# Up-projections of the last feed-forward part as seven block products on halves of 256 columns

## The chip, the cores and the metric

The program runs on one core of a Trainium2 chip. A core has TensorE (PE, matrix products; its weight loads are shown apart as PEld), VectorE (DVE), ScalarE (ACT), GpSimd (POOL) and SyncE (SP, which here only issues DMA transfers). The engines run side by side, each strictly in the order of its own instruction list, and wait for each other through semaphores. The metric is the device time of one execution in microseconds, median of three runs. One execution was also profiled; all rows come from that one.

## The reference

Two layers of a diffusion backbone over 512 latent tokens and 256 context tokens, width 1024, in float32. Each layer is a half feed-forward part, a token mixer, and a second half feed-forward part. The last part of the last layer runs on the 512 latent tokens alone:

```python
def half_ffn(x, shift, scale, gate, w_in, w_out, g, b):
    h = modulate(x, shift, scale)
    a, u = jnp.split(h @ w_in, 2, axis=-1)
    y = (jax.nn.silu(a) * u) @ w_out
    return layernorm(ALPHA * x + 0.5 * gate * y, g, b)
...
        x_lat = half_ffn(x_lat, m_lat[6], m_lat[7], m_lat[8], ffn_w_in[l, 1], ffn_w_out[l, 1], ln_g[l, 2], ln_b[l, 2])
```

`w_in` is 1024 x 5632 and `w_out` 2816 x 1024. 2816 is 22 chunks of 128.

## The kernel before

**Tiling.** Activations are kept transposed: 128 features on the partitions, 8 chunks of features (`KC`), tokens along the free dimension. Every operand of a product is split into a high and a low part (`HHI`, `HLO` for the activations, `WHI*`, `WLO*` or `WSH`, `WSL` for weights), and a product of one 128 x 128 weight block is three matmuls: high x high, high x low, low x high (`product`, L3103 to 3111). ACT makes the high parts by a copy that rounds, DVE the low parts by a subtraction.

**Feed-forward parts.** There are four, `ffn0` to `ffn3`. Each has eleven iterations (`FI`), and each iteration has a unit A and a unit B (one chunk of 128 hidden features each, gate and up). A unit is: the up-projection on PE, silu on ACT, the multiplication by the up half on DVE, and the split into `GHI`, `GLO`. The down-projection of iteration i-1 runs in iteration i; DVE adds each of its results into `X` (`accumulate`).

**The last part, `ffn3`, before.** It uses the plain form (`ffn`, with S = 1). Per iteration PE runs up A (48 matmuls of 512 columns), the whole down-projection (8 groups of 6 matmuls, 512 columns) and up B (48). Weights come in six transfers of 512 KB per iteration through two raw buffers (`RAW[0]`, `RAW[1]`, printed as RAW): transfer q may be issued when transfer q-2 has been split (`lo_done`).

**The other three parts** use the block form (`wide`). In iterations 2 to 10 the up-projection of a unit, an [8 chunks of features] x [768 tokens] product with two outputs (gate, up), is cut into halves in all three directions and computed by seven block products instead of eight (`seventh`: 4 k-steps x 3 matmuls on 384 columns each), with sums of activation blocks (`TH_`, `TL_`, made once per part in iterations 0 to 2) and with mixes of weight blocks, made per unit. Each unit's results are put together on DVE (`second_sum`, `gate_first`, `third_sum`, `fourth_sum`, `up_second`, `up_first`, `gate_second`). The weights for the next unit are made while this one runs, in one buffer `WSH`/`WSL` of seven places:

- DVE mixes in place in the raw buffers: `difference`, `total`, `mix_second`, `last_mix` (L2220 to 2248), 512 columns each.
- ACT makes the high parts: `raw_hi` (1024 columns, L1246), four `mix_hi` (L1253) and `second_hi` (L1259), 512 columns each.
- DVE makes the low parts: `low_first` (1024 columns, L2217) and five of 512 columns, the last being `low_last` (L2256), which frees both raw buffers at once (`lo_done` + 2).

The raw buffers are used in turn by a half of `w_out` rows (`rows_load`, L736), then the first and the second half of the next unit's up weights (`unit_load`, L714). The rows and the first half may be issued when `low_last` of the unit before is done; the second half uses the buffer of the rows, so it is issued when DVE has split the rows (L1802, called `rows()` in `unit`). Down-projections are spread: half of the groups after unit A, half after unit B. The order on each engine is written out by hand in `unit` and `body` of each engine's block.

Of the kernel before, what the change touches and what calls it, by code (L numbers as in the profile page):

```python
# [167 lines left out]
def build(nc, A, out):  # L168
# [197 lines left out]
    RST = sb("RST", [P, LAT // P], at=r2 + 8192)  # L366
    OUT = sb("OUT", [P, LAT // P, D], F32, at=w_at)
# [93 lines left out]
    ffn_plan("ffn3", 1)  # L461
# [91 lines left out]
    BLOCKS = {"ffn0": 0, "ffn1": 1, "ffn2": 2}  # L553
# [18 lines left out]
    def fourth_sums(name, k):  # L572

        return T4S[k][:, :, :] if name == "ffn2" else HL32[:, 2 * k:2 * k + 2, HALF:TOK]

    def blocks_of(part):

        H = (HHI, HLO)[part]
        T = (TH_, TL_)[part]
        return {"11": lambda k: H[:, k, 0:HALF], "21": lambda k: H[:, 4 + k, 0:HALF], "22": lambda k: H[:, 4 + k, HALF:TOK],  # L580
                "T4": lambda k: H[:, k, HALF:TOK], "T1": lambda k: T[1][k // 2][:, k % 2, :],
                "T2": lambda k: T[2][k // 2][:, k % 2, :], "T3": lambda k: T[3][k // 2][:, k % 2, :]}
# [13 lines left out]
    def half_bank(a, m):  # L596

        return PS[(1, 0)[m - 4] if a == 0 and m in (4, 5) else (6, 7, 2, 5)[m % 4]][:, 0:CTX]
# [87 lines left out]
    def _(sp):  # L686
# [28 lines left out]

        def ffn(name, w_in, w_out):
            q0 = plan[name].q
            for half in range(2):
                ffn_load(w_in, w_out, "A", 0, half, q0 + half)

            def body(i, last=False):
                for slot, d, half, j in ffn_halves(last):
                    ffn_load(w_in, w_out, slot, i + d, half, q0 + j, i)
            with sp.Fori(0, FI - 1) as i:
                body(i)
            body(FI - 1, last=True)
# [145 lines left out]
        ffn("ffn3", A["ffn_w_in"][1, 1], A["ffn_w_out"][1, 1])  # L872
# [216 lines left out]
    def _(act):  # L1089
# [57 lines left out]
        def ffn(name, S, ada, nxt):  # L1147
            p = plan[name]

            used = {"A": (p.A, S), "B": (p.B, S), "W": (p.W, KC * S)}  # L1150

            def free_value(slot, u):
                base, per = used[slot]
                if isinstance(u, int) and base + per * u == 0:
                    return None
                return base + per * u

            def silus(slot, i):

                b = 0 if slot == "A" else 3  # L1160
# [33 lines left out]
            for e, s in enumerate(ORDER[2]):  # L1194
# [4 lines left out]
                if e == 0:  # L1199
                    next_unit(nxt, "A")  # L1200
# [2777 lines left out]
```

## Time and profile before

| | us |
|---|---|
| median of three runs | 2800.71 (2800.42 to 2800.82) |
| the profiled execution | 2798.63 |
| its span, first to last instruction | 2796.9 |
| PE busy | 2767.4 (99%) |
| DVE busy | 1988.9 (71%) |
| ACT busy | 1041.6 (37%) |

A row of a timeline gives start, duration, engine, line, operation and operands; in brackets the idle time of the engine just before, and what ended it. A matmul's duration is longer than the distance to the next one, since they are pipelined, so the cost of a matmul in a dense stretch is the distance between starts. The same holds, by less, for DVE and ACT. Iterations 1 to 10 of `ffn3` lie between about 2440 and 2766.5 us of the span, and the steady half-iterations of `ffn2`, the block form without other work in it, at about 1700 to 1950 us.

### The profile page before, as it was taken

To read this page: it belongs to the slowest core of one execution; us is meant where nothing else is said; L and a number is where in the kernel's file an instruction comes from. 1 tells how busy PE (TensorE), PEld (TensorE's weight loads), DVE (VectorE), ACT (ScalarE), POOL (GpSimd) and SP (SyncE) were. 2 spreads that over 40 slices of the span, in tenths; PEclk is the share of its full clock that TensorE was granted. 3 is DMA by queue.
4 is the path that set the end of the run, shared out by engine and by line. 5 is a ranking of instruction groups with operands and counts; after the bars stand their busy time and mean duration, and the time that the engine had idled before them with its cause. 6 is when DMAs were issued, how large, how long until landed. Compare 5 with 4: busy or idle time off the path is not lost.

```text
span 2796.9 us, 46107 instructions
## 1 busy us (share of the span) xinstructions
PE 2767.4 (99%) x17150; PEld 2423.9 (87%) x17150; DVE 1988.9 (71%) x3249; ACT 1041.6 (37%) x1646; POOL 296.2 (11%) x404
## 2 busy tenths in 40 slices
PE   8999999999999999999999999999999999999999
PEld 4899989988868889999898999999978998988888
DVE  5786777776785777667677877777767886655555
ACT  4232323346632523323234333333356665522221
POOL 2000000011101000000001000000105554000000
PEclk9999999999999999999999999999999999999999
DMA  9344342222222243443421112222311101232221
GB/s 340 106 158 158 120 142 68 68 68 76 69 102 84 77 156 129 157 152 125 142 83 43 56 69 70 72 71 71 86 43 26 27 21 46 85 119 95 100 90 61
DMA packets 112292, 268.00 MB, mean 96 GB/s; under 512 B 30760, under 2 KB 40876, under 8 KB 112045
## 3 DMA queue, kind: packets, MB, share of 16 engines
q1 hardware_dynamic: 89164, 185.62, 20.5%
q0 software_dynamic: 22144, 77.61, 7.8%
q10 hardware_dynamic: 864, 3.15, 0.3%
q8 instruction: 79, 1.29, 0.2%
q14 instruction: 41, 0.33, 0.0%
HBM read 259.52 MB, written 5.24 MB: 95 GB/s over the span
## 4 chain that ended last, share of the span: by engine, by line
PE 93%; DVE 3%; ACT 2%; DMA 1%; issue 1%; POOL 0%; ACTq 0%; DVEq 0%; POOLq 0%; SPq 0%
PE PSALL L3109 15%; PE PSALL L3110 15%; PE PSALL L3111 15%; PE PSALL L3399 9%; PE PSALL L3400 9%; PE PSALL L3401 9%; PE PSALL L3185 2%; PE PSALL L3024 2%; PE PSALL L3186 2%; PE PSALL L3187 2%; PE PSALL L3862 2%; PE PSALL L3847 1%; PE PSALL L3138 1%; PE PSALL L3808 1%; PE PSALL L3810 1%
## 5 line engine op out<-in xcount | busy, mean ns | idle before, releaser
L2146 DVE SCALAR_TENSOR_TENSOR X<-PSALL,GATE,X 128x512 f32<-128x512 f32 x480 | 280.1, 612 | 94.5 <-PE PSALL L3111 94.5
L3399 PE MATMUL PSALL<-HHI,WSH 128*128 128x384 f32 x864 | 291.2, 337 | 0.0
L3400 PE MATMUL PSALL<-HLO,WSH 128*128 128x384 f32 x864 | 290.2, 336 | 0.0
L3401 PE MATMUL PSALL<-HHI,WSL 128*128 128x384 f32 x864 | 289.8, 335 | 0.0
L1253 ACT ACTIVATE WSH<-RAW 128x512 fp32r<-128x512 f32 x216 | 136.6, 632 | 228.7 <-DVE RAW L2223 152.6
L3399 PE MATMUL PSALL<-TH,WSH 128*128 128x384 f32 x648 | 220.3, 340 | 0.0
L3401 PE MATMUL PSALL<-TH,WSL 128*128 128x384 f32 x648 | 218.9, 338 | 0.0
L3400 PE MATMUL PSALL<-TL,WSH 128*128 128x384 f32 x648 | 218.9, 338 | 0.0
L3109 PE MATMUL PSALL<-GHIA,WHIW 128*128 128x512 f32 (+1 forms) x570 | 198.5, 348 | 0.6 <-DVE X L2146 0.6
L3110 PE MATMUL PSALL<-GLOA,WHIW 128*128 128x512 f32 (+1 forms) x570 | 196.6, 345 | 0.0
L3111 PE MATMUL PSALL<-GHIA,WLOW 128*128 128x512 f32 (+1 forms) x570 | 196.0, 344 | 0.0
L3111 PE MATMUL PSALL<-GHIB,WLOW 128*128 128x512 f32 (+1 forms) x570 | 195.8, 343 | 0.0
L3109 PE MATMUL PSALL<-GHIB,WHIW 128*128 128x512 f32 (+1 forms) x570 | 195.7, 343 | 0.0
L3110 PE MATMUL PSALL<-GLOB,WHIW 128*128 128x512 f32 (+1 forms) x570 | 195.6, 343 | 0.0
L3109 PE MATMUL PSALL<-HHI,WHIA 128*128 128x512 f32 (+1 forms) x464 | 167.2, 360 | 0.0
L3110 PE MATMUL PSALL<-HLO,WHIA 128*128 128x512 f32 (+1 forms) x464 | 165.3, 356 | 0.0
L3111 PE MATMUL PSALL<-HHI,WLOA 128*128 128x512 f32 (+1 forms) x464 | 165.3, 356 | 0.0
L3399 PEld LDWEIGHTS PSALL<-HHI,WSH 128*128 128x128 f32 x864 | 162.3, 188 | 0.4 <-issue 0.4
L3400 PEld LDWEIGHTS PSALL<-HLO,WSH 128*128 128x128 f32 x864 | 162.5, 188 | 0.0
L3401 PEld LDWEIGHTS PSALL<-HHI,WSL 128*128 128x128 f32 x864 | 162.2, 188 | 0.0
L3109 PE MATMUL PSALL<-HHI,WHIB 128*128 128x512 f32 (+1 forms) x432 | 155.9, 361 | 0.0
L3111 PE MATMUL PSALL<-HHI,WLOB 128*128 128x512 f32 (+1 forms) x432 | 154.6, 358 | 0.0
(443 smaller groups left out, 6829.6 us busy)
## 6 DMA issues: line engine op xcount, KB each, us to landing
RAW<-in_ffn_w_in_dram SPq DMA_DIRECT2D x174, 512.0 KB, 3.8
ADA<-in_ada_w_dram POOLq DMA_DIRECT2D x128, 512.0 KB, 5.6
RAW<-in_ffn_w_out_dram SPq DMA_DIRECT2D x88, 512.0 KB, 3.6
RAW<-in_ev_w_in_dram SPq DMA_DIRECT2D x20, 512.0 KB, 3.7
ADAF<-in_ada_w_dram POOLq DMA_DIRECT2D x16, 512.0 KB, 12.0
WRAW<-in_mla_w_q_up_dram SPq DMA_DIRECT2D x16, 288.0 KB, 3.1
RAW<-in_ev_w_out_dram SPq DMA_DIRECT2D x8, 512.0 KB, 4.5
RAW<-in_mla_w_in_dram SPq DMA_DIRECT2D x8, 512.0 KB, 4.0
```

Of the source, the lines that this page charges most:

```text
L1253: return act.activation(WSH[:, place, :], raw[:, 512 * cols:512 * cols + 512], ACT.Copy)
L2146: dve.scalar_tensor_tensor(X[:, m, lo:lo + n], down_bank(m, s, 2), GATE[:, j, m, s:s + 1], X[:, m, lo:lo + n], ALU.mult, ALU.add).then_inc ...
L3024: x = te.matmul(PS[bank][32 * j:32 * j + 32, 0:D // 4], SC[:, k, :], rows[:, j * D // 4:(j + 1) * D // 4], start=(k == 0), stop=(k == KC - 1))
L3109: te.matmul(out, w_hi, x_hi(k), start=(k == 0), stop=False)
L3110: te.matmul(out, w_hi, x_lo(k), start=False, stop=False)
L3111: x = te.matmul(out, w_lo, x_hi(k), start=False, stop=(k == ks - 1))
L3185: te.matmul(out, hi, HHI[:, k, lo:lo + n], start=(k == 0), stop=False)
L3186: te.matmul(out, hi, HLO[:, k, lo:lo + n], start=False, stop=False)
L3187: return te.matmul(out, low, HHI[:, k, lo:lo + n], start=False, stop=(k == KC - 1))
L3399: te.matmul(out, w_hi, hi[block](k), start=(k == 0), stop=False)
L3400: te.matmul(out, w_hi, low[block](k), start=False, stop=False)
L3401: x = te.matmul(out, w_lo, hi[block](k), start=False, stop=(k == 3))
```

## The change

`ffn3` takes the block form in iterations 2 to 10, on halves of 256 columns instead of 384. Iterations 0 and 1 stay plain (`up_classic`). The plain `ffn` functions are replaced on every engine by `narrow`, which follows `wide` line by line, without the context tokens; SP uses `wide` as it is. Down-projections keep 512 columns and are spread, four groups after each unit. The high part of the gated result moves from DVE to ACT. In the last iteration the down rows get a third buffer of their own (`WL3H`, `WL3L`).

```diff
-    ffn_plan("ffn3", 1)
+    stage("ffn3", q=6 * FI, A=2 * FI, B=2 * FI, W=KC * FI, evac=KC * FI, g=FI, gB=FI, gs=2 * FI)
...
-        ffn("ffn3", A["ffn_w_in"][1, 1], A["ffn_w_out"][1, 1])
+        wide("ffn3", A["ffn_w_in"][1, 1], A["ffn_w_out"][1, 1])
...
+            def unit(slot, i, rows, q):
...
+                first_copy(slot, i)
+                rows()
+                silu_first(slot, i)
+                raw_hi(n, q, i, (g_pe, 5 * v + 3))
+                mix_hi(n, 1, 2, first, 0, (g_pe, 5 * v + 4)).then_inc(g_hi, 1)
+                mix_hi(n, 2, 3, second, 0, (g_pe, 5 * v + 5)).then_inc(g_hi, 1)
+                second_hi(n, q, i, (pe[slot], used + 1))
+                silu_second(slot, i)
+                mix_hi(n, 3, 4, second, 1, (g_pe, 5 * v + 2)).then_inc(g_hi, 1)
+                mix_hi(n, 4, 5, first, 1, (pe[slot], used + 2)).then_inc(hi_done, 2)
...
+                def low_first():
+                    dve.wait_ge(g_hi, 5 * n + 1)
...
+                def difference():
+                    dve.wait_ge(raw_in[raw_slot(q + 1)], raw_value(q + 1, i))
+                    dve.wait_ge(g_lo, 5 * n + 1)
+                    dve.tensor_tensor(first[:, left], first[:, left], second[:, left], ALU.subtract).then_inc(g_mix, 1)
...
+            def up(slot, i, q):
...
+                te.wait_ge(mul[slot], p.gs + 2 * i)
+                te.wait_ge(g_lo, 5 * v + 1)
+                seventh(0, "11", b).then_inc(g_pe, 1)
+                te.wait_ge(g_lo, 5 * v + 5)
+                te.wait_ge(t_lo, 8 * blk + 6)
+                seventh(4, "T2", b + 1).then_inc(g_pe, 1)
+                seventh(1, "21", b + 2).then_inc(g_pe, 1)
+                te.wait_ge(g_p1, v + 1)
+                seventh(2, "T3", b).then_inc(g_pe, 1)
+                te.wait_ge(g_add, 7 * v + 1)
+                seventh(3, "T1", b + 1).then_inc(g_pe, 1)
+                te.wait_ge(g_add, 7 * v + 2)
+                te.wait_ge(t_lo, 8 * blk + 7)
+                seventh(6, "T4", b + 2, lambda: te.wait_ge(t_lo, 8 * blk + 8)).then_inc(pe[slot], 1)
+                te.wait_ge(g_add, 7 * v + 3)
+                te.wait_ge(lo_done, q + 2 + 6 * i)
+                seventh(5, "22", b).then_inc(pe[slot], 1)
...
+                for m in groups:
+                    if m >= 2:
+                        te.wait_ge(evac, p.evac + KC * i + m - 1)
...
+            def body(i):
+                up("A", i, wide_q(name, "A", 1) - 6)
+                down(i - 1, range(0, 4), wide_q(name, "W0", 1) + 6 * i - 6 + 1)
+                up("B", i, wide_q(name, "B", 1))
+                down(i - 1, range(4, 8), wide_q(name, "W1", 1) + 6 * i + 1)
```

The order on VectorE, iteration 1 of `ffn3` before, from the multiplication of unit B on (GM, GHI, GLO are the gated result and its parts, WLOB, WLOA low parts of weights, RAW_54 and RAW_53 the two raw buffers, X the residual stream):

```order
L1990 TENSOR_TENSOR GMB<-GMB,PSALL 128x512 [waits silu_B,ln_x]
L2000 CAST GHIB<-GMB 128x512 [waits mul_B]
L2002 TENSOR_TENSOR GLOB<-GMB,GHIB 128x512 [waits ghi_B]
L1802 TENSOR_TENSOR WLOB<-RAW_54,WHIB 128x1024 [waits hi_done]
L2015 SCALAR_TENSOR_TENSOR X<-PSALL,GATE,X 128x512 [waits pe_W]
L1802 TENSOR_TENSOR WLOB<-RAW_53,WHIB 128x1024 [waits hi_done]
L1990 TENSOR_TENSOR GMA<-GMA,PSALL 128x512 [waits silu_A]
L2015 SCALAR_TENSOR_TENSOR X<-PSALL,GATE,X 128x512 [waits pe_W] x3
L1802 TENSOR_TENSOR WLOA<-RAW_54,WHIA 128x1024 [waits hi_done]
```

And in the changed kernel, the same engine in unit A of the last iteration, which has the order of the steady ones, from the split of the rows to the end of the weights for the next unit (seven_hi, seven_mix the counts of high parts and mixes, raw_in1 the landing of a transfer):

```order
L1873 TENSOR_TENSOR WLOW<-RAW_54,WHIW 128x1024 [waits hi_done]
L2101 TENSOR_TENSOR GMA<-PSALL,P_95 128x256 [waits seven_pe]
L2156 TENSOR_TENSOR WSL<-RAW_53,WSH 128x1024 [waits seven_hi]
L2110 TENSOR_TENSOR U_96<-PSALL,GMA 128x256 [waits seven_add,seven_pe,mul_B]
L2162 TENSOR_TENSOR RAW_53<-RAW_53,RAW_54 128x512 [waits seven_lo,raw_in1]
...
L2141 TENSOR_TENSOR GMA<-PSALL,GMA 128x256 [waits pe_A]
L2183 TENSOR_TENSOR RAW_54<-RAW_54,RAW_53 128x512 [waits seven_mix,seven_lo]
L2187 TENSOR_TENSOR RAW_53<-RAW_53,RAW_54 128x512 [waits seven_mix]
L2146 TENSOR_TENSOR GMA<-GMA,P_95 128x256 [waits silu_A]
L2077 SCALAR_TENSOR_TENSOR X<-PSALL,GATE,X 128x512 [waits evac,pe_W] x2
L2191 TENSOR_TENSOR WSL<-RAW_54,WSH 128x512 [waits seven_hi]
L2077 SCALAR_TENSOR_TENSOR X<-PSALL,GATE,X 128x512 [waits evac,pe_W]
L2195 TENSOR_TENSOR WSL<-RAW_53,WSH 128x512 [waits hi_done]
```

Where each weight tile was split by itself, there is now one chain of mixes and splits, and accumulations of the down-projection stand between its last members. On SyncE the loop of `ffn3` issued, for each iteration, two transfers for unit B, two for unit A and two of rows:

```order
L714 ISA [waits lo_done]
L714 DMA RAW_54<-in_ffn_w_in_dram 128x1024
...
L714 DMA RAW_53<-in_ffn_w_in_dram 128x1024
...
L714 DMA RAW_54<-in_ffn_w_in_dram 128x1024
...
L714 DMA RAW_53<-in_ffn_w_in_dram 128x1024
...
L714 DMA RAW_54<-in_ffn_w_out_dram 128x1024
```

In the loop of the changed kernel each unit's pair is followed by one transfer of rows:

```order
L717 ISA [waits lo_done]
L717 DMA RAW_53<-in_ffn_w_in_dram 128x1024
...
L717 DMA RAW_54<-in_ffn_w_in_dram 128x1024
...
L727 DMA RAW_53<-in_ffn_w_out_dram 128x2x512
...
L717 DMA RAW_54<-in_ffn_w_in_dram 128x1024
...
L717 DMA RAW_53<-in_ffn_w_in_dram 128x1024
```

So the second transfer of each pair takes the buffer that the rows before it held.

## Rows read from the trace of the kernel before

**Rows 1.** The page: span, busy times, granted clock by slice, the chain's engines.

```profile
span 2796.9 us, 46107 instructions
PE 2767.4 (99%) x17150; PEld 2423.9 (87%) x17150; DVE 1988.9 (71%) x3249; ACT 1041.6 (37%) x1646; POOL 296.2 (11%) x404
...
PEclk9999999999999999999999999999999999999999
...
PE 93%; DVE 3%; ACT 2%; DMA 1%; issue 1%; POOL 0%; ACTq 0%; DVEq 0%; POOLq 0%; SPq 0%
```

**Rows 2.** Busy times of 100 us inside `ffn3` (stretch, length, busy, granted clock, DMA).

```profile
2500.00:2600.00 100.00, 100.00 (x443) 82.84 (x442) 48.19 (x60) 20.99 (x24) 0.00 (x0) 1.00 0.31 101
```

**Rows 3.** PE timeline: 512-column matmuls in `ffn3`, the first and the 56th.

```profile
2559.81 0.39 PE L3109 MATMUL PSALL<-HHI,WHIB 128*128 128x512 f32 x1
...
2572.28 0.39 PE L3110 MATMUL PSALL<-HLO,WHIA 128*128 128x512 f32 x1
```

**Rows 4.** PE timeline: last down-projection; 256-column matmuls, the first and the 24th.

```profile
2766.53 0.28 PE L3299 MATMUL PSALL<-GHIA,WHIW 128*128 128x256 f32 x1
...
2771.55 0.28 PE L3109 MATMUL PSALL<-GHIA,WHIW 128*128 128x256 f32 x1
...
2774.31 0.28 PE L3111 MATMUL PSALL<-GHIB,WLOW 128*128 128x256 f32 x1
```

**Rows 5.** DVE timeline of `ffn2`, one half-iteration of the block form.

```profile
1860.20 0.68 DVE L2256 TENSOR_TENSOR WSL<-RAW,WSH 128x512 fp32r<-128x512 f32 x1
...
1868.11 1.22 DVE L1802 TENSOR_TENSOR WLOW<-RAW,WHIW 128x1024 fp32r<-128x1024 f32 x1
...
1873.45 0.68 DVE L2223 TENSOR_TENSOR RAW<-RAW,RAW 128x512 f32<-128x512 f32 x1
1874.05 0.56 DVE L2179 TENSOR_TENSOR GMA<-PSALL,GMA 128x384 f32<-128x384 f32 x1
...
1880.59 1.40 DVE L2146 SCALAR_TENSOR_TENSOR X<-PSALL,GATE,X 128x512 f32<-128x512 f32 x2
1881.91 0.68 DVE L2252 TENSOR_TENSOR WSL<-RAW,WSH 128x512 fp32r<-128x512 f32 x1
1882.51 0.87 DVE L2146 SCALAR_TENSOR_TENSOR X<-PSALL,GATE,X 128x256 f32<-128x256 f32 x2
1883.30 0.68 DVE L2256 TENSOR_TENSOR WSL<-RAW,WSH 128x512 fp32r<-128x512 f32 x1
```

**Rows 6.** ACT and SP timelines of the same half-iteration.

```profile
1865.90 1.05 ACT L1144 ACTIVATE WHIW<-RAW 128x1024 fp32r<-128x1024 f32 x1
...
1861.06 0.38 SPq L736 DMA_DIRECT2D RAW<-in_ffn_w_out_dram  x1
...
1869.50 0.33 SPq L714 DMA_DIRECT2D RAW<-in_ffn_w_in_dram  x1
```

**Rows 7.** Time from issue to landing, 1650 to 2000 us: rows, then up weights.

```profile
DMA to landing us min/median/max: 3.5/3.7/4.7
...
DMA to landing us min/median/max: 3.4/3.8/4.5
```

**Rows 8.** DVE groups by shape, from 2420 us on.

```profile
L2015 DVE SCALAR_TENSOR_TENSOR X<-PSALL,GATE,X 128x512 f32<-128x512 f32 x80 | 58.4, 748 | 22.8 <-PE PSALL L3111 22.8
...
L1919 DVE TENSOR_TENSOR X<-X,PSALL 128x256 f32<-128x256 f32 x16 | 5.9, 414 | 1.0 <-PE PSALL L3128 0.7 <-PE PSALL L3146 0.4
```

**Rows 9.** PE timeline of the kernel's start, around an idle time of 3.4 us.

```profile
16.23 1.08 PE L3024 MATMUL PSALL<-ADAF,SC 128*32 128x256 f32 x8 [3.40 <-DMA ADAF<-in_ada_w_dram]
...
20.95 0.73 PE L3024 MATMUL PSALL<-ADAF,SC 128*32 128x256 f32 x8
...
26.15 0.64 PE L3024 MATMUL PSALL<-ADAF,SC 128*32 128x256 f32 x8
```

More of the change, by code:

```diff
@@ L552, in build @@
     UNITS = 2 * (FI - 2)
[L553 removed]
+    BLOCKS = {"ffn0": 0, "ffn1": 1, "ffn2": 2, "ffn3": 3}
     def wide_q(name, kind, i):
@@ new lines, in unit @@
+            def unit(slot, i, q, rows, groups):
+                low_first, difference, total, low_difference, low_total, low_second, mix_second, last_mix, low_third, low_last = weights(q, i, seven(name, slot, i) + 1)
+                second_sum(slot, i)
+                rows()
+                gate_first(slot, i)
+                low_first()
+                third_sum(slot, i)
+                difference()
+                fourth_sum(slot, i)
+                up_second(slot, i)
+                total()
+                low_difference()
+                up_first(slot, i)
+                low_total()
+                gated_first(slot, i)
+                low_second()
+                gate_second(slot, i)
+                mix_second()
+                last_mix()
+                gated_second(slot, i)
+                for e in groups[:2]:
+                    accumulate(i - 1, e)
+                low_third()
+                accumulate(i - 1, groups[2])
+                low_last()
+                accumulate(i - 1, groups[3])
@@ new lines, in narrow @@
+            low_first, difference, total, low_difference, low_total, low_second, mix_second, last_mix, low_third, low_last = weights(wide_q(name, "A", 1), 1, seven(name, "A", 2))
+            accumulate(0, 0)
+            accumulate(0, 1)
+            block_sum(1, 1)
+            accumulate(0, 2)
+            block_sum(1, 3)
+            accumulate(0, 3)
+            block_sum(1, 2)
+            for n in (1, 3, 2):
+                block_difference(1, n)
+            low_first()
+            difference()
@@ L2116, in wide @@
+            for m in range(KC):
+                center(then, 1, 1, m)
         def wide(name, j, ada, t0, then, nxt, tables=None):
@@ new lines, in up_classic, with seventh @@
+                x.then_inc(pe[slot], 2)
+            def seventh(place, block, bank, half_way=None):
+                out = PS[bank][:, 0:CTX]
+                for k in range(4):
+                    w_hi, w_lo = (t[:, place, P * k:P * k + P] for t in (WSH, WSL))
+                    if half_way and k == 2:
+                        half_way()
+                    te.matmul(out, w_hi, hi[block](k), start=(k == 0), stop=False)
+                    te.matmul(out, w_hi, low[block](k), start=False, stop=False)
+                    x = te.matmul(out, w_lo, hi[block](k), start=False, stop=(k == 3))
+                return x
@@ L3363, in wide @@
+            sums(then, 1, 1, lambda m: e0 + KC + m + 1)
         def wide(name, ada, ln, then):
```

627 lines of the change are left out of this document (355 added, 272 removed).

## The prediction

> **What bounds the kernel now.** I read the page first: PE is busy 99% of the span, the granted clock reads full in every slice, and the chain that ended last is 93% PE [rows 1]. Then the stretch that the change touches: for 100 us inside `ffn3` PE is busy all the time, DVE 48%, ACT 21%, the DMA engines 31% [rows 2]. So here the number of matmuls, times the distance between two of them, is the time. The next view is the PE timeline, read for distances: 512 columns cost (2572.28 - 2559.81) / 55 = 0.2267 us [rows 3], 256 columns (2774.31 - 2771.55) / 23 = 0.1200 us [rows 4]. One iteration is 3 x 48 matmuls of 512 columns, 32.64 us, or 16.32 us for a half-iteration (one unit and half of a down-projection). The nine iterations that the change rewrites take 18 x 16.32 = 293.8 us and end where the last down-projection starts, at 2766.53 [rows 4].
>
> The second place to read is the steady part of `ffn2`, since it is the form that `ffn3` takes over. One half-iteration there runs from 1860.20 to 1883.30, the two starts of `low_last`: 23.10 us [rows 5]. What matters is not that PE is full there too, but the loop that runs beside it, below.
>
> **What the change takes from PE.** A unit was 48 x 0.2267 = 10.88 us; it becomes 7 x 12 = 84 matmuls of 256 columns, 84 x 0.1200 = 10.08 us. The down-projection keeps 24 x 0.2267 = 5.44 us per half-iteration. PE's work per half-iteration falls from 16.32 to 15.52 us, by 0.80; over 18 it is 14.4 us. Halving the columns saves 12.5% of the columns, but each matmul costs 0.013 us beyond its columns (twice 0.1200 less 0.2267), and there are 84 instead of 48, which leaves 7%.
>
> The Trainium skill, "TensorE: Matmul & The Clock Gate", section "Back-to-back issue gap", gives N/2.4 + 2.5 ns as the isolated distance of one matmul of N columns, which would be 109 and 216 ns; an estimate from it is a saving of 1.2 us per half-iteration, 21.6 us in all. Rows 3 and 4 show 120 and 227 ns for these split products, and the measured distances decide.
>
> **What it adds beside PE.** DVE work per half-iteration, in distances between starts: 256 columns 0.335 (duration 0.414 [rows 8], less the 0.08 by which an operation overlaps the next: 1873.45 to 1874.05 is 0.60 for a duration of 0.68 [rows 5]), 512 columns 0.60, 1024 columns 1.14, an accumulation 0.66 (1.40 for two, less the same 0.08 [rows 5]). Nine block sums and multiplications 3.0, four mixes and five low parts 5.5, two low parts of 1024 columns 2.3, four accumulations 2.7, the low part of the gated result 0.6: 14.1 us. Below 15.5, so as work it fits; ACT fits easily (some 8 us). What does not fit is the order.
>
> **The loop.** The weights of the next unit pass through two raw buffers, and each step waits for the one before. Followed once around, from the end of `low_last`:
> 1. SP issues the rows: 1861.06 against 1860.20 + 0.68 = 1860.88, so 0.18 us [rows 5, 6]. Landing takes 3.5 at least, 3.7 in the median [rows 7]: I take 3.6.
> 2. ACT makes the high part of the rows, 1.05 [rows 6]; DVE the low part, 1.22 [rows 5]. With 0.05 before each, 2.37.
> 3. That frees the buffer for the second half of the next weights: issued at 1869.50 against 1868.11 + 1.22, 0.17 [rows 5, 6], landing 3.4 at least, 3.8 in the median, for one alone less than for one of two in flight [rows 7]: I take 3.55. With steps 1 and 2: 0.18 + 3.6 + 2.37 + 0.17 + 3.55 = 9.9 us in which DVE can't go on to `difference`.
> 4. From `difference` to the end of `low_last` DVE goes through its list: 1873.45 to 1883.98, 10.53 us [rows 5]. Six of these operations have 384 columns (0.555 for the `fourth_sum`, [rows 5]) and will have 256 (0.414 [rows 8]), 0.14 less each, 0.8 in all; two accumulations of 256 columns (0.79 apart, 1882.51 to 1883.30 [rows 5]) become one of 512 (0.66). That gives 9.6.
> 5. Before `low_last` stands the accumulation of the third down group. In the changed kernel this group may start only when the first is accumulated (`evac`, one bank pair): first accumulation 0.75 [rows 8], group 1.36, pipeline end 0.16, against 1.92 that DVE needs to get there. DVE waits about 0.4.
>
> The loop is 9.9 + 9.6 + 0.4 = 19.9 us. It does not depend on PE's speed. In `ffn2` the same count gives 9.9 + 10.5 = 20.4, and PE needs 23.1, so it is hidden; there ACT starts on the rows only at 1865.90 [rows 6], well after they landed, as it first waits for PE. In `ffn3` PE needs 15.5, and the loop becomes the pace: +3.6 us per half-iteration against 16.32, where 0.80 was to be won. PE will wait in two places: before the seventh block product, which needs `third_sum`, queued on DVE behind `low_first`, which needs the rows split and the gate sum (about 1.2 us), and before the third down group, whose bank waits for an accumulation that is queued behind the late mixes (about 3 us).
>
> **The sum.** 18 half-iterations, of which the last makes no weights for a next one. 17 x 19.9 = 338.3. The last has splits of two row blocks but no mixes; I take 18.2, between PE's 15.5 and the loop's 19.9. Entry: iterations 0 and 1 get 12 sums and differences of activation blocks, six low parts and ten operations for the fourth block, 512 columns each, 28 x 0.60 = 17 us of DVE. Part lies in DVE's idle half, but the first accumulation of iteration 1 stands behind nine of them and a transfer, about 4 us late, and the ten for the fourth block stand right ahead of the first new unit: 6 us, of which some 3.3 lie in the time the rows take to land. I take 4.8 + 2.7 = 7.5 us. The last down-projection (96 matmuls of 256 columns) and the layer norm stay: 0. After: 338.3 + 18.2 + 7.5 = 364.0, against 293.8: **+70.2 us**. The span becomes 2867.1. The profiled run was 1.7 above its span of 2796.9 [rows 1] and the median of three 3.8 above it (table of times); the difference goes on the median: 2800.7 + 70.2 = **2870.9**.
>
> Bounds of the unknown terms: the loop with the least landings, 3.5 and 3.4, and no wait of step 5 is 9.65 + 9.6 = 19.2; with both landings 0.5 longer 20.9. Entry 0 to 12, last half-iteration 15.5 to 20. Low end 17 x 19.2 + 15.5 - 293.8 = +48.1, 2849; high end 355.3 + 20 + 12 - 293.8 = +93.5, 2894.
>
> **The rivals.**
> - *PE keeps the pace, faster.* If landings, splits and mixes for one unit overlapped those of the next, the 15.52 us of PE work would set the time: -14.4 us, or 2786 with nothing lost at the entry, 2794 with the 7.5 there. The loop would have to be 3.6 us shorter than the rows add up to before the change is even neutral (16.32). For it: in `ffn2` the form runs without any wait of PE, and DVE's 14.1 us fit. Against it: each step has a semaphore and only two buffers, and `low_last` frees both at once.
> - *The clock falls too.* The wait before the third down group comes to some 3 to 3.5 us each half-iteration. At the kernel's start PE waits 3.40 us, and eight matmuls of 256 columns then take 1.08 us, later 0.64 [rows 9]: close to a factor of two, so 1.2 instead of 2.4 GHz, though the granted clock's row reads full [rows 1]. With each third group at half speed the loop's step 5 grows by 1.36: 17 x 1.36 = 23 us, 2894. For it: the length is near to that one. Against it: PE was not warm before that early wait either, and two waits per 20 us leave it 78% busy. The Trainium skill, in the same page, section "HAM oscillation", warns that gaps between bursts bring the low clock back every time; by that rule this rival would be the result.
> - *The loop closes, but shorter.* If DVE's operations run closer or the rows land earlier, 17.5 us: +29 with the entry, 2830.
> - That the change doesn't do what it says: the seven calls of `seventh` in the diff are 84 matmuls of 256 columns per unit, so this has no chance of its own.
>
> **Chances.** The forecast 0.76 (its own range 2849 to 2894), the clock 0.12, a shorter loop 0.06, PE's pace 0.05, something near 16.3 per half-iteration 0.01. The range for 8 in 10 is 2848 to 2896: it takes the forecast's bounds and the lighter half of the clock case. 0.2% is 5.6 us, about what a measurement can tell from no change: faster 0.05, within 0.01, slower 0.94.
>
> **What would show it.** In the changed profile: PE busy in `ffn3` down to about 78%; the starts of `low_last` 19.9 us apart; idle time of ACT before the rows' high part put down to DMA, and of DVE before `difference` to DMA; PE waiting for DVE `X` before a down matmul, about 3 us each; 84 matmuls per unit 0.120 us apart. Wrong would be: starts of `low_last` at 15.5 or 16 us, DVE waiting for PE as now, or matmuls of 256 columns some 0.22 us apart behind the waits (the clock).

## The result and the profile after

The changed kernel takes 2889.29 us (median of 4 runs, 2887.45 to 2890.45) against 2800.57 before: ratio 1.0317, 95% interval 1.0299 to 1.0335. The forecast was 2870.9 with a range of 2848 to 2896. The kernel before was run again beside this one, so its time differs by 0.1 us from the one in the table ahead of the prediction.

The page of the profiled execution, the lines that answer to [rows 1]: span, busy times, clock by slice, the chain's engines.

```profile
span 2888.7 us, 48461 instructions
PE 2784.1 (96%) x17798; PEld 2458.9 (85%) x17798; DVE 2123.2 (73%) x3545; ACT 1106.6 (38%) x1780; POOL 296.2 (10%) x404
...
PEclk9999999999999999999999999999999999899999
...
PE 80%; DVE 8%; DMA 6%; issue 3%; ACT 2%; POOL 0%; DVEq 0%; SPq 0%; ACTq 0%; POOLq 0%
```

The chain that ended last is 80% PE instead of 93%; DVE and DMA have come into it. Two stretches of 50 us inside `ffn3` (length, busy PE, PEld, DVE, ACT, POOL, granted clock, DMA share, GB/s), to set beside [rows 2]:

```profile
2500.00:2550.00 50.00, 40.01 (x238) 34.99 (x237) 35.49 (x63) 15.95 (x27) 0.00 (x0) 0.93 0.19 63
2550.00:2600.00 50.00, 41.20 (x291) 37.85 (x289) 33.19 (x57) 16.52 (x26) 0.00 (x0) 1.00 0.28 90
```

PE is busy 80% and 82% where it was busy 100%, and the granted clock is below full in the first stretch. What the engines waited for from 2500 to 2850 us (total, times, longest):

```profile
PE PSALL L3372 <- DVE X L2077: 50.4, 17, 3.2
...
ACT WHIW L1135 <- DMA RAW<-in_ffn_w_out_dram: 28.8, 18, 2.4
...
PE PSALL L3509 <- DVE U L2110: 11.5, 12, 1.4
...
DVE RAW L2162 <- DMA RAW<-in_ffn_w_in_dram: 7.1, 16, 0.6
```

L3372 is the first matmul of a product in a down group (the wait is that before the third group), L2077 an accumulation; L1135 the high part of the rows; L3509 the seventh block product, L2110 `third_sum`; L2162 `difference`; L3373 and L3374, below, are the second and third matmul of a product. Now one half-iteration on DVE, from one `low_last` (L2195) to the next, as in [rows 5]; the split of the rows is L1873, `low_first` L2156, `low_third` L2191.

```profile
2549.93 0.68 DVE L2195 TENSOR_TENSOR WSL<-RAW,WSH 128x512 fp32r<-128x512 f32 x1
...
2555.56 1.23 DVE L1873 TENSOR_TENSOR WLOW<-RAW,WHIW 128x1024 fp32r<-128x1024 f32 x1 [1.64 <-ACT WHIW L1135]
...
2560.64 0.69 DVE L2162 TENSOR_TENSOR RAW<-RAW,RAW 128x512 f32<-128x512 f32 x1 [0.53 <-DMA RAW<-in_ffn_w_in_dram]
...
2566.99 1.40 DVE L2077 SCALAR_TENSOR_TENSOR X<-PSALL,GATE,X 128x512 f32<-128x512 f32 x2
2568.30 0.68 DVE L2191 TENSOR_TENSOR WSL<-RAW,WSH 128x512 fp32r<-128x512 f32 x1
2569.56 0.75 DVE L2077 SCALAR_TENSOR_TENSOR X<-PSALL,GATE,X 128x512 f32<-128x512 f32 x1 [0.58 <-PE PSALL L3374]
2570.23 0.68 DVE L2195 TENSOR_TENSOR WSL<-RAW,WSH 128x512 fp32r<-128x512 f32 x1
```

The same stretch on ACT and on SP's queue:

```profile
2554.47 1.06 ACT L1135 ACTIVATE WHIW<-RAW 128x1024 fp32r<-128x1024 f32 x1 [2.09 <-DMA RAW<-in_ffn_w_out_dram]
...
2550.80 0.38 SPq L727 DMA_DIRECT2D RAW<-in_ffn_w_out_dram  x1
2551.46 5.84 SPq L717 DMA_DIRECT2D RAW<-in_ffn_w_in_dram  x2
```

The loop can be followed through these rows: `low_last` ends at 2550.61, the rows are issued at 2550.80 and have landed at 2554.47, are split by 2556.79, the second half of the next weights lets `difference` start at 2560.64, and the next `low_last` ends at 2570.91: 20.30 us. In [rows 6] ACT reached the rows late because it waited for PE; here it waits 2.09 us for their transfer.

In all there are 18 starts of `low_last`, from 2483.05 to 2839.79. The first step is 24.71 us; of the other sixteen ten are 20.1 to 20.8 and the rest 20.8 to 21.8.

Of the two waits that were forecast for PE, the one before the third down group stands in each half-iteration and the one before the seventh block product in 12 of them. Behind the first of these two the clock differs from loop to loop:

```profile
2560.25 0.38 PE L3509 MATMUL PSALL<-HHI,WSH 128*128 128x256 f32 x1 [1.13 <-DVE U L2110]
...
2567.78 0.50 PE L3372 MATMUL PSALL<-GHIA,WHIW 128*128 128x512 f32 x1 [3.10 <-DVE X L2077]
...
2568.82 0.39 PE L3373 MATMUL PSALL<-GLOB,WHIW 128*128 128x512 f32 x1
2569.05 0.39 PE L3374 MATMUL PSALL<-GHIB,WLOW 128*128 128x512 f32 x1
...
2671.53 0.50 PE L3372 MATMUL PSALL<-GHIA,WHIW 128*128 128x512 f32 x1 [2.87 <-DVE X L2077]
...
2672.78 0.63 PE L3373 MATMUL PSALL<-GLOB,WHIW 128*128 128x512 f32 x1
2673.21 0.63 PE L3374 MATMUL PSALL<-GHIB,WLOW 128*128 128x512 f32 x1
```

The granted clock of PE in 3 us of each of these two groups:

```profile
2568.00:2571.00 3.00, 3.00 (x16) 1.00 0.00 0
2672.00:2675.00 3.00, 3.00 (x10) 0.55 0.00 0
```

512 columns are 0.23 us apart at 2.4 GHz and 0.43 at 1.2 GHz, behind waits of nearly the same length. What this costs can be read on DVE: from `difference` to `low_last` it is 9.5 to 9.6 us in nine of the 17 steps, 9.9 to 10.6 in five, and 10.86 in the three in which the granted clock is 0.50 for the whole 3 us from the start of the third group.

### The profile page after: what moved, and what is told of

It is laid out like the page before. It is cut to its first block, busy times and chain, and to the rows that moved or that the text cites. A ratio compares the mean times of both kernels' runs of the same rounds, so it can differ in the third digit from the quotient of the medians.

```text
span 2888.7 us, 48461 instructions
## 1 busy us (share of the span) xinstructions
PE 2784.1 (96%) x17798; PEld 2458.9 (85%) x17798; DVE 2123.2 (73%) x3545; ACT 1106.6 (38%) x1780; POOL 296.2 (10%) x404
## 3 DMA queue, kind: packets, MB, share of 16 engines
q1 hardware_dynamic: 91980, 185.62, 19.9%
q10 hardware_dynamic: 864, 3.15, 0.3%
q8 instruction: 81, 1.33, 0.2%
## 4 chain that ended last, share of the span: by engine, by line
PE 80%; DVE 8%; DMA 6%; issue 3%; ACT 2%; POOL 0%; DVEq 0%; SPq 0%; ACTq 0%; POOLq 0%
PE PSALL L3372 12%; PE PSALL L3374 11%; PE PSALL L3373 11%; PE PSALL L3625 9%; PE PSALL L3626 9%; PE PSALL L3627 9%; DMA RAW<-in_ffn_w_out_dram 3%; DMA RAW<-in_ffn_w_in_dram 2%; PE PSALL L3287 2%; PE PSALL L3448 2%; PE PSALL L3449 2%; PE PSALL L3450 2%; PE PSALL L4088 1%; PE PSALL L4073 1%; PE PSALL L3401 1%
## 5 line engine op out<-in xcount | busy, mean ns | idle before, releaser
L3372 PE MATMUL PSALL<-GHIA,WHIW 128*128 128x512 f32 (+1 forms) x560 | 201.3, 359 | 59.7 <-DVE X L2077 58.6
L3373 PE MATMUL PSALL<-GLOA,WHIW 128*128 128x512 f32 (+1 forms) x560 | 197.2, 352 | 0.0
L3374 PE MATMUL PSALL<-GHIA,WLOW 128*128 128x512 f32 (+1 forms) x560 | 196.7, 351 | 0.0
L3372 PE MATMUL PSALL<-GHIB,WHIW 128*128 128x512 f32 (+1 forms) x560 | 196.4, 351 | 0.0
L3374 PE MATMUL PSALL<-GHIB,WLOW 128*128 128x512 f32 (+1 forms) x560 | 196.3, 351 | 0.0
L3373 PE MATMUL PSALL<-GLOB,WHIW 128*128 128x512 f32 (+1 forms) x560 | 196.3, 351 | 0.0
L3372 PEld LDWEIGHTS PSALL<-GHIA,WHIW 128*128 128x128 f32 x560 | 107.5, 192 | 85.5 <-DVE X L2077 67.2
L920 POOL TENSOR_TENSOR RSTD<-X 128x256 f32<-128x256 f32 (+1 forms) x12 | 12.0, 998 | 1412.1 <-DVE X L2648 805.5
L880 POOL DMA_DIRECT2D ADA<-in_ada_w_dram x128 | 67.6, 528 | 791.2 <-PE PSALL L3287 673.3
L1873 DVE TENSOR_TENSOR WLOW<-RAW,WHIW 128x1024 fp32r<-128x1024 f32 x90 | 110.5, 1229 | 40.6 <-ACT WHIW L1135 40.6
L1135 ACT ACTIVATE WHIW<-RAW 128x1024 fp32r<-128x1024 f32 x92 | 96.7, 1054 | 86.7 <-DMA RAW<-in_ffn_w_out_dram 75.2
```

What stands on the lines that cost most here:

```text
L880: pool.dma_start(ADA[slot][:, :], ada_rows(l, k, group)).then_inc(ada_in[slot], 16)
L1135: act.activation(WHI[slot][:, 1024 * half:1024 * half + 1024], RAW[raw_slot(q)][:, :], ACT.Copy).then_inc(hi_done, 1)
L1873: dve.tensor_tensor(WLO[slot][:, cols], RAW[raw_slot(q)][:, :], WHI[slot][:, cols].bitcast(F32), ALU.subtract).then_inc(lo_done, 1)
L3372: te.matmul(out, w_hi, x_hi(k), start=(k == 0), stop=False)
L3373: te.matmul(out, w_hi, x_lo(k), start=False, stop=False)
L3374: x = te.matmul(out, w_lo, x_hi(k), start=False, stop=(k == ks - 1))
```

## The experiments

Theory L: in `ffn3` the time is set by the loop through the two raw buffers, 20.3 us against PE's 15.5. Its rivals: D, the DVE operations as such (their sum) are too much; P, PE's waits for the accumulations are what costs; C, the low clock behind the waits. The first column of the table is the label, the steps are worked out from the starts of `low_last`. The kernel before was measured again beside the runs, with medians from 2799.37 to 2800.57, so a difference of about 1 us between two rows means nothing.

| run | us | ratio to before (95%) | first step | mean of the other 16 |
|---|---|---|---|---|
| changed kernel | 2889.29 | 1.0299 to 1.0335 | 24.71 | 20.75 |
| e1_rows_apart | 2872.29 | 1.0244 to 1.0278 | 24.09 | 19.72 |
| e2_last_low_first | 2873.46 | 1.0247 to 1.0282 | 22.67 | 19.84 |
| e3_work_outside | 2890.88 | 1.0308 to 1.0342 | 24.54 | 20.88 |
| e4_work_inside | 2903.87 | 1.0360 to 1.0394 | 24.85 | 21.54 |
| e5_rows_and_second_half | 2853.80 | 1.0176 to 1.0210 | 23.42 | 18.67 |
| e6_reordered | 2809.17 | 1.0018 to 1.0043 | 23.10 | 15.95 |
| e7_reordered_shared | 2894.32 | 1.0320 to 1.0355 | 23.66 | 21.06 |
| e8_fill_wait | 2883.96 | 1.0282 to 1.0317 | 23.92 | 20.41 |
| e9_entry | 2800.29 | 0.9994 to 1.0012 | 18.33 | 15.82 |
| e10_copy_first | 2868.45 | 1.0232 to 1.0263 | 23.72 | 19.40 |
| e11_entry_and_end | 2799.71 | 0.9990 to 1.0008 | 18.72 | 15.82 |
| e12_entry_alone | 2883.81 | 1.0287 to 1.0319 | 20.58 | 20.67 |

**Rows in a buffer of their own.**

```diff
             def rows_load(half, u, q, i=0, own=False):
-                sp.wait_ge(lo_done, q - 1 + 6 * i)
-                sp.dma_start(RAW[raw_slot(q)][:, :]...
+                sp.wait_ge(lo_done, q - (2 if own else 1) + 6 * i)
+                sp.dma_start((ROWS3 if own else RAW[raw_slot(q)])[:, :]...
```

> The rows of the down-projection get a raw buffer of their own in ffn3 from iteration 1 on, and are loaded as soon as DVE has split the rows before them. Order on every engine unchanged. Theory L (the loop through the two raw buffers sets the pace): the pair for the next unit can be issued at once when low_last is done, the 9.9 us of row transfer, split and second transfer leave the loop, and a half-iteration falls from 20.3 to about 18.1 us, where DVE, ACT and PE wait for each other in their written order: 17 x 2.2 = 37 us less, 2852 us (2844 to 2860). Rival D (the amount and order of DVE's work sets the pace, transfers are hidden): no change, 2886 to 2892.

Measured: 17 us off, not 37, and not zero either. The trace of this run, SP's queue and DVE:

```profile
2546.86 5.95 SPq L718 DMA_DIRECT2D RAW<-in_ffn_w_in_dram  x2
...
2551.07 1.22 DVE L2299 TENSOR_TENSOR WLOW<-ROWS,WHIW 128x1024 fp32r<-128x1024 f32 x1
...
2556.13 0.69 DVE L2173 TENSOR_TENSOR RAW<-RAW,RAW 128x512 f32<-128x512 f32 x1 [0.51 <-DMA RAW<-in_ffn_w_in_dram]
```

The second of the two transfers is issued only when the split of the rows is over (2552.29). I had kept the wait of the second half as it was, so that only the rows' transfer left the loop. That the loads matter is shown; that they are the whole is not yet.

**One operation moved within the loop.**

```diff
                 low_third()
-                accumulate(i - 1, groups[2])
                 low_last()
+                accumulate(i - 1, groups[2])
                 accumulate(i - 1, groups[3])
```

> DVE makes low_last before the accumulation of the third down group instead of after it. Theory L: low_last no longer waits for the third down group on PE (nor for that group at half clock), and starts one accumulation earlier, so the loop gets about 1.1 us shorter: 17 x 1.15 = 20 us less, 2869 us (2862 to 2876). Rival P (PE's waits for down banks are what costs): the third accumulation comes 0.6 us later, PE's next groups with it, 5 to 10 us more, 2894 to 2899. Rival D: the amount of DVE work is the same, no change.

Measured 2873.5, 16 off. From `difference` to `low_last` it is 8.26 us in each of the sixteen steps, 1.33 less than where the clock stays up and 1.7 less than the mean of 9.97; the mean step falls by 0.9 only. The rest went into the stretch behind it: from `low_last` to the split of the rows 6.6 us on average instead of 5.8, because the rows' high part stands on ACT behind the copy of PE's first product, and PE still has its last two down groups to do. Rival P falls: the third accumulation, for which PE waits, now stands one operation later, and the time fell.

**The same work outside and inside.** One more DVE operation of 512 columns, whose result is not used, ahead of `second_sum`, where DVE waits anyway, or ahead of the accumulations.

```diff
+                dve.tensor_tensor(SPARE[:, :], HHI[:, 4, 0:LAT].bitcast(F32), HLO[:, 4, 0:LAT].bitcast(F32), ALU.add)
```

> One more DVE operation of 512 columns (0.6 us) per unit, its result unused, ahead of second_sum, where the loop waits for the rows to land and be made. Theory L: it fits in that wait, no change (2886 to 2892). Rival D: DVE's work sets the pace, 17 x 0.6 = 10 us more, 2899.

> The same extra DVE operation of 512 columns, but between gated_second and the accumulations, between difference and low_last. Theory L: each loop gets 0.60 us longer, 17 x 0.6 = 10 us more, 2899 (2896 to 2903). Rival D: the same 10 us, so this run alone doesn't tell them apart, only beside the one with the operation outside. Rival P (PE or its clock sets the pace): less than 5 us.

Outside, 1.6 us more than the changed kernel, with overlapping intervals: no change that these runs can tell, where D asked for 10. Inside, +14.6 us, and 13.0 more than outside in runs made side by side, where one operation per loop makes 10; it lies just above the expected 2896 to 2903. `difference` to `low_last` is 10.2 where the clock stays up (+0.6, as expected) and up to 11.5 where it falls. The excess over the undisturbed value adds up to 11 us in the sixteen steps, against 6 in the changed kernel, and that is where the other 5 us are. So it is not the sum of DVE's work but the work between two `low_last`: D falls, L stands.

**Both transfers freed from the split.**

```diff
-                sp.wait_ge(lo_done, q - 1 + 6 * i)
+                sp.wait_ge(lo_done, q - (2 if own and half else 1) + 6 * i)
```

> As the first experiment (the rows of the down projection in a buffer of their own), and the second half of each up-projection pair is requested as soon as the last low part of the pair before it is written, no longer behind the split of the rows; iteration 1 of the SP queue is written out for that. In the first experiment the profile showed that this second half still waited for the rows' split (issued 0.2 us behind its end), so that only one of the two transfers had left the loop. Theory L (the period is the loop low_last, both halves' transfer, difference, ten VectorE and ScalarE steps, low_last): the rows' split leaves the loop whole, which is then landing about 4, wait to the difference and 9.6 to 10.5 us: about 18.1 us for 20.3, so 17 x 2.2 = 37 us off: 2852 us, 20 below the first experiment. Theory P (what is left is set by TensorE's own wait for the accumulations, not by the loads): 2870 to 2874, as the first experiment.

Measured 2853.8. SP's queue now issues the pair at once:

```profile
2583.53 0.87 SPq L718 DMA_DIRECT2D RAW<-in_ffn_w_in_dram  x2
...
2587.93 0.38 SPq L729 DMA_DIRECT2D ROWS<-in_ffn_w_out_dram  x1
```

The steps mostly alternate between 18.0 to 18.5 and 18.8 to 19.4 us, mean 18.67 where 18.1 was expected. So the loads were part of the loop. From `low_last` to `difference` it is still 8.9 us (10.8 in the changed kernel), but from 2510 to 2800 us of this trace no engine waits for a transfer any more. What is left is the waits of DVE, ACT and PE for each other, and so the order of their operations, which the next run changes.

**Another order.** The work of a half-iteration rearranged on ACT (first part) and on DVE, none added, on top of the run before.

```diff
-                first_copy(slot, i)
                 rows()
-                silu_first(slot, i)
+                if slot == "A":
+                    gate_hi("B", i - 1)
+                first_copy(slot, i)
...
+                silu_first(slot, i)
                 second_hi(n, q, i, (pe[slot], used + 1))
...
                 second_sum(slot, i)
-                rows()
                 gate_first(slot, i)
-                low_first()
+                if slot == "A":
+                    gate_low("B", i - 1)
+                rows()
                 third_sum(slot, i)
+                low_first()
...
                 low_total()
+                accumulate(i - 1, groups[0])
                 gate_second(slot, i)
+                accumulate(i - 1, groups[1])
+                low_second()
                 mix_second()
                 last_mix()
-                gated_second(slot, i)
-                for e in groups[:2]:
-                    accumulate(i - 1, e)
                 low_third()
-                accumulate(i - 1, groups[2])
                 low_last()
+                accumulate(i - 1, groups[2])
+                gated_second(slot, i)
                 accumulate(i - 1, groups[3])
```

> As the run before, and VectorE and ScalarE work in another order in a half-iteration: first gate sum ahead of the rows' split, two of the four accumulations ahead of the last weight mixes instead of all four around them, the last low part ahead of the third and fourth accumulation, ScalarE's first raw split ahead of the SiLU. No work is added or removed. Theory L: the loop through the buffers shrinks below TensorE's own 15.5 us, so that TensorE sets the period, with waits of some tenths: about 16 us each, 17 x (21.0 - 16.0) = 85 us off the 2889: about 2804 us, and the 3 us waits ahead of the third down group are gone. Theory V (VectorE's own work of 14.1 us with its latencies is the bound once the loads are free): 17.5 to 18 us, 2840 to 2850.

Measured 2809.2, 5 above what was expected. The starts of `low_last` are 15.6 to 16.1 us apart (the last 17.2), PE's own pace. Two hundred us inside `ffn3`, to set beside [rows 2]:

```profile
2500.00:2700.00 200.00, 198.27 (x1358) 182.14 (x1357) 183.62 (x313) 83.34 (x137) 0.00 (x0) 1.00 0.29 97
```

DVE is busy 92% and still not the bound (rival V of the expectation, DVE's own work), and the clock is full.

The same order without the own buffer, that is, on the changed kernel itself:

> The order of the run before alone, with the two raw buffers shared as in the changed kernel. Theory L: the loop goes through the rows' transfer still, but the steps between are shorter: about 17 us, 2889 - 17 x 4 = 2821 us. If the two loads in a row were the whole cost, and the order only its cover, 2880 or more.

Measured 2894.3: 73 us above what L gave, and 5 above the changed kernel. The number lies in the other branch, but not for its reason. The waits from 2520 to 2750 us:

```profile
ACT WHIW L1135 <- DMA RAW<-in_ffn_w_out_dram: 48.8, 11, 5.0
...
PE PSALL L3509 <- ACT P L1159: 32.0, 11, 3.4
```

L1159 is ACT's copy of the first product. In the new order it stands behind the rows' high part. With an own buffer the rows have long landed there; with the shared ones ACT waits up to 5.0 us for them, and PE for the copy. The order that is right with one set of buffers is wrong with the other. The run `e10_copy_first` puts that copy, and in unit A the high part of the gated result with it, back in front of the rows; here its edit against `e7_reordered_shared`:

```diff
-                rows()
+                first_copy(slot, i)
                 if slot == "A":
                     gate_hi("B", i - 1)
-                first_copy(slot, i)
+                rows()
```

> The reordering with the two raw buffers shared, but on ScalarE the copy of the first product's bank stays ahead of the rows' split, as in the changed kernel. In the run with the shared buffers and both engines reordered (2894 us) the profile showed ScalarE's copy standing behind the rows' split, which waited up to 5.0 us for its transfer, and TensorE waiting up to 3.4 us for that copy. Theory A (that ScalarE order made the 2894; without it the reordered VectorE helps also with shared buffers, but the rows' transfer stays in the loop, so the loop doesn't fall below two landings and the steps between): about 19 us a loop, 17 x 1.8 to 2.1 = 30 to 36 us off the 2889: 2853 to 2860. Theory B (the ScalarE order was harmless): 2890 to 2895.

Measured 2868.5, 26 us less than with the copy behind, and 21 less than the changed kernel. It lies outside both of the expected ranges, but far nearer to the first: the loss of `e7` came from what stood behind the rows on ACT, and its trace names the copy as what PE waited for. The steps are 19.4 on average where 19 was expected, of which 8.65 from `difference` to `low_last` (9.6 in the changed kernel) and, as in the changed kernel, 5.8 to the split of the rows and 5.0 to `difference`. The buffers alone give 35 us. DVE's new order alone gives 21 with ACT's copy left in front, and costs 5 in the form of `e6`; that form with the buffers gives 80. The copy left in front together with the own buffers was not run.

**Filling PE's wait.**

```diff
                 for m in groups:
+                    if m == groups[2] and not isinstance(i, int):
+                        for _ in range(20):
+                            te.matmul(PS[5 if m == 2 else 2][:, CTX:LAT], rows[0][:, m // 4, 0, m % 4, :], GHI["A"][:, 0:CTX], ...
```

> The changed kernel, with 20 matmuls of 256 columns (2.4 us at full clock) on data that is already there, written to half a bank that nobody reads, ahead of TensorE's wait before the third down group of each half-iteration, in the nine looped iterations. Their result is not used. Theory C (the loops of 20.7 to 21.7 us, against 20.3 of the others, are longer because the granted clock falls behind the 3 us wait): every loop comes to 20.3, about 7 us off: 2882 us. Theory N (the added matmuls cover nothing and end before the wait does): 2887 to 2891, with the steps as they were. If they push the group behind them: above 2895.

Measured 2884.0, and all but the last of the sixteen steps, which the filled loop doesn't hold, are 20.1 to 20.6. PE in one of them, and 200 us inside `ffn3`:

```profile
2564.18 2.55 PE L3547 MATMUL PSALL<-GHIA,WHIW 128*128 128x256 f32 x20
2567.26 0.50 PE L3372 MATMUL PSALL<-GHIA,WHIW 128*128 128x512 f32 x1 [0.53 <-DVE X L2077]
```

```profile
2500.00:2700.00 200.00, 182.62 (x1270) 168.89 (x1269) 142.72 (x246) 67.38 (x110) 0.00 (x0) 1.00 0.23 76
```

The waiting time is the same, with other work in it, and the granted clock is 1.00 (0.93 in the changed kernel over the same stretch). So the low clock is not what sets the pace: with it gone the steps are still 20.4 us. What it costs the changed kernel is about 5 us by this run (4.2 when each is taken against the kernel before as measured beside it), and 8 at most by the steps, as added up below.

**The way in.** After `e6` PE still waits where iterations 0 and 1 are:

```profile
2460.83 0.80 PE L3396 MATMUL PSALL<-GHIA,WHIW 128*128 128x512 f32 x1 [5.10 <-DVE X L2095]
...
2492.02 0.58 PE L3533 MATMUL PSALL<-TH,WSH 128*128 128x256 f32 x1 [2.89 <-DVE GMA L2113]
```

```diff
             split_lo("B", 0, q, 1)
+            accumulate(0, 0)
             split_lo("B", 1, q + 1, 1)
+            accumulate(0, 1)
             blocks_low(0)
...
+            fourth_first(0)
+            fourth_rest(0)
             low_first()
...
             low_second()
+            fourth_first(1)
+            fourth_rest(1)
+            accumulate(0, 4)
```

> The reordered version with the rows in a buffer of their own and the freed second half, plus a shorter way in and out of the nine iterations; nothing is computed otherwise. On VectorE, in iterations 0 and 1: the accumulations of the first two down groups ahead of the block products' low parts (TensorE waited 5.1 us there), the sums of the fourth block (four double columns of work, 6.5 us in a row ahead of the first block unit, for which TensorE waited 2.9 us) moved into the idle time of iteration 1, the accumulation of the fifth group one step earlier (wait 1.5 us), and the eight scalings of the last norm's gains moved from ahead of the last iteration into its idle time (TensorE waits of 0.3 and 1.0 us). Theory E (those waits are paid in full because TensorE is the pace everywhere behind them): 3.5 + 1.3 + 2.5 + 1 = about 8 us off the 2809: 2801 us, within 0.2% of the kernel before. Theory O (each of the waits only uncovers another: 2805 to 2809).

Measured 2800.3, within 0.2% of before. But one of the waits only moved, as its PE timeline shows:

```profile
2476.84 0.80 PE L3399 MATMUL PSALL<-GHIA,WHIW 128*128 128x512 f32 x1 [5.23 <-DVE X L2095]
```

> On top of the reordered version with the shorter way in: its trace still shows TensorE waiting 5.2 us for the accumulation of the fifth group in iteration 1 (the wait of 5.1 us that was taken away ahead of the first group has moved there, because the fourth block's sums stood ahead of it on VectorE), and 1.9 us for the same accumulation in the last half-iteration. Here both accumulations stand three to five steps earlier, and the last sums of the fourth block are done within the first block unit, ahead of its sixth product. Theory E: VectorE is busy nearly without a break in iteration 1, so of the 5.2 us only about 2 come back; with the 1.9 at the end 3 to 4 us off: 2796 to 2798. Theory O: nothing comes back in iteration 1 (VectorE's own work sets its length), 1.9 at the end: 2798 to 2799.

Measured 2799.7, ratio 0.9999: less gain than either branch expected. Its profiled execution is 3.8 us shorter than that of `e9`, its PE timeline has 0.76 us in place of the 5.23, and new waits in other places:

```profile
2471.66 0.50 PE L3413 MATMUL PSALL<-GHIA,WHIW 128*128 128x512 f32 x1 [0.76 <-DVE X L2095]
...
2484.16 0.36 PE L3550 MATMUL PSALL<-HHI,WSH 128*128 128x256 f32 x1 [1.33 <-DVE HLO L2307]
...
2492.19 0.50 PE L3413 MATMUL PSALL<-GHIA,WHIW 128*128 128x512 f32 x1 [1.90 <-DVE X L2095]
```

The medians of eleven runs each show 0.6 us of it. Whether the 3 us are there is left open.

The same rearrangement in the changed kernel, with its loop as it is:

> The changed kernel with its loop as it is, and only the way in and out of the nine iterations rearranged as in the ninth run (first two accumulations ahead of the block products' low parts, the fourth block's sums spread over iteration 1, the last norm's gains in the last iteration). Theory E (the first loop step of 24.7 us is 4.4 us longer than the undisturbed 20.3 because the ten operations on the fourth block, 6.5 us, stand ahead of its unit, and the first low_last is late by TensorE's 5 us wait): the first step falls to 20.5 to 21.5 and the first low_last comes 1 to 2 us earlier: 5 to 6 us off: 2883 to 2884. Theory S (the loop is set by the transfers, which start at the first low_last whatever stands behind it): the first step stays above 23 us, and only 1 to 2 us come off: 2887 to 2888.

Measured 2883.8, 5.5 off (4.6 when each is taken against the kernel before as measured beside it), and the first step is 20.58. Eight of the ten operations on the fourth block have left it, and from `low_last` to the split of the rows it is 5.7 us instead of 9.4: that stretch was theirs. The accumulations were moved in the same run, and the first `low_last` comes only 0.8 us earlier, counted from the first gating operation of `ffn3`, because PE's wait of 5 us has moved here too (5.22 us at 2477.35).

## Why the prediction was right, point by point

The mechanism held, the size was 18.4 us short. The measured time lies inside the range with 7 us to spare at its upper end, and it is nearer to the clock rival's 2894 than to the forecast's 2870.9, though the clock makes less than half of the difference. Three terms were each too small, in the loop, the clock and the entry, and nothing of any size made up for them; that the range held them all owes something to luck. By the steps:

- *PE's own work, 15.52 us per half-iteration*: right. In `e6` and `e9`, where nothing else sets the pace, the steps are 15.6 to 16.1 (one of 17.2), mean 15.95 and 15.82. The saving of 0.8 us per half-iteration is therefore real, some 0.5 of it in practice. The distances of [rows 3] and [rows 4] were the right price; by the formula that the Trainium skill gives ("TensorE: Matmul & The Clock Gate", "Back-to-back issue gap") a half-iteration would be 84 x 0.109 + 24 x 0.216 = 14.3 us, an estimate, and no step of any run came below 15.5.
- *Steps 1 to 3 of the loop, 9.9 us*: measured 2550.61 to 2560.64, 10.03.
- *Steps 4 and 5, 9.6 and 0.4*: measured 10.27 with a wait of 0.58. The loop is 20.3 instead of 19.9: over 17 steps 6.8 us of the miss.
- *The clock*, a rival with 23 us and no term in the sum: right in kind, wrong in how often. What lies above 20.3 in the sixteen steps is 356.74 - 24.71 - 16 x 20.3 = 7.2 us, of which 6.0 are between `difference` and `low_last`. A third group at low clock throughout makes that stretch 10.86 instead of 9.60, 1.26 us where 1.36 was forecast; but this came in full in three steps of 17 and in part in five, where the rival had it in all. One of the signs of being wrong did show, in one place: behind the wait of 3.15 us in the first unit, below, matmuls of 256 columns are 0.21 us apart. The Trainium skill ("TensorE: Matmul & The Clock Gate", "HAM oscillation") describes a kernel in which waits of about 3 to 5 us bring the low clock back every time. The prediction left that length out and called this rival the result by that rule; the waits here, 2.9 to 3.2 us in the sixteen steps, lie at its short end and had the low clock behind them in some loops only, and one of 2.12 us in the first step had it too.
- *Entry, 4.8 + 2.7*: under-sized. The first step is 4.4 too long (24.71 less 20.3) instead of 2.7, and up to the first `low_last` 8.6 us are lost instead of 4.8 (92.55 - 17 x 3.98 - 7.2 - 4.4, less 2.4 for the later start and 2.3 for the last half-iteration, both below). PE waits 5.00 and 1.54 us there, and for 2 us behind the first of these waits the granted clock is 0.50. Together 5.5 us of the miss. The step that failed: I counted the fourth block's ten operations as hidden by the rows' landing for 3.3 us, but `second_sum`, on which PE waits, stands behind all ten, and so does the split of the rows:

```profile
2461.17 0.80 PE L3372 MATMUL PSALL<-GHIA,WHIW 128*128 128x512 f32 x1 [5.00 <-DVE X L2077]
...
2480.69 0.50 PE L3372 MATMUL PSALL<-GHIA,WHIW 128*128 128x512 f32 x1 [1.54 <-DVE X L2077]
...
2492.59 0.58 PE L3509 MATMUL PSALL<-TH,WSH 128*128 128x256 f32 x1 [3.15 <-DVE GMA L2095]
```

```profile
2483.05 0.68 DVE L2195 TENSOR_TENSOR WSL<-RAW,WSH 128x512 fp32r<-128x512 f32 x1
...
2490.30 0.69 DVE L2282 TENSOR_TENSOR HLO<-HL,HHI 128x512 fp32r<-128x512 f32 x1
...
2492.12 0.42 DVE L2095 TENSOR_TENSOR GMA<-PSALL,P 128x256 f32<-128x256 f32 x1
2492.45 1.22 DVE L1873 TENSOR_TENSOR WLOW<-RAW,WHIW 128x1024 fp32r<-128x1024 f32 x1
```

  L2282 is the last of the ten, L2095 `second_sum`. From `low_last` to the split it is 9.4 us where 5.8 is the mean of the other steps, so the ten cost 3.6. The other 0.8 of the 4.4 lie between `difference` and `low_last` (10.42), where the granted clock is 0.59 in the 3 us from the start of the third group: with the 7.2 above, the clock comes to 8.0 us in all.
- *Last half-iteration, 18.2*: 2840.47 to 2859.08, 18.6.
- *Around it*: `ffn3` begins 2.4 us later in this execution, the tail is 0.8 shorter, and the median lies 0.6 above the profiled span instead of 3.8.

Together: 6.8 + 7.2 + 5.5 + 0.4 + 2.4 = 22.3 at the start of the last down-projection (2859.08 against 2766.53 is +92.55, forecast +70.2), less 0.8 and 3.2.

PE's two waits came as forecast, 3.0 us on average (50.4 / 17) before the third down group and 1.0 (11.5 / 12), where it occurs, before the seventh product. Of the rivals, "PE keeps the pace" is false for this kernel and true for `e6`: it needed what the forecast named, the loads and mixes of one unit no longer in one chain with those of the next. And even then it does not win: with the entry paid, 18 x 0.5 us are gone again in iterations 0 and 1, and `e9` and `e11` end where the kernel before ends.

## What to carry to other kernels

When a stage takes over a form that runs without waits elsewhere, look for the loop through its shared buffers and add it up on its own, transfers and every queued operation in between: what was hidden behind 23.1 us of PE work was 20 us long and became the pace where PE needs 15.5. To shorten such a loop, free the buffers first and then sort the queues for it: own buffers alone gave 35 us, with the new order 80. That order without them cost 5 us, and one copy put back in front turned this into a gain of 21. And before starting, weigh what is to be won against the way in: here 14 us by the forecast and 9 as it ran, against 13 us of preparation as first written, and the 9 again after it was rearranged.

## What was not expected of the hardware

- The granted clock did not fall in every loop: 1.00 and 0.55 behind waits of 3.10 and 2.87 us. In the 20 us that hold the loop ahead of each (2548 to 2568, 2652 to 2672), PE was busy 79% and 85%: it was the busier one that had the low clock behind it, though part of those 85% is itself work at low clock. In `e8`, with PE busy 91%, it stayed at 1.00 for 200 us. What decides it between these is open.
- Kernels whose program is the same up to `ffn3` enter it at different times in their single profiled executions: its first gating operation starts at 2438.89 in the changed kernel, 2436.58 in `e4` and 2440.31 in `e8`. A difference of 3 us between two traces is no finding; the medians are needed.
- In `e6` DVE, busy 92%, still kept PE at 99%: a DVE near full is no reason against a change, if its queue is in the right order.
